# Seven block products move from the down-projection to 19 pairs of the up-projection, with two half-depth down units inside each step

## The reference, cut to what matters

```
h2 = rmsnorm(x, norm2_g)
up, new_conv_f = causal_dwconv(jnp.einsum('btd,df->btf', h2, w_up), ffn_conv0, conv_f_w, conv_f_b)
gf, vf = jnp.split(up, 2, axis=-1)
x = x + jnp.einsum('btf,fd->btd', jax.nn.gelu(gf) * vf, w_down)
```

## Time and profile before

| what | value |
|---|---|
| time, median of 3 runs | 1156.68 us (1156.22 to 1157.01) |
| time of the profiled execution | 1157.05 us |
| its span (first to last instruction or transfer) | 1155.3 us |
| TensorE busy | 1149.3 us, 99% of the span |
| VectorE busy | 663.3 us, 57% |
| ScalarE busy | 542.7 us, 47% |
| GpSimd busy | 245.5 us, 21% |
| feed-forward part on TensorE | from about 698 us to the end |

### The profile page before, as it was taken

The page is one execution under the profiler, slowest core; times in us unless marked ns, Lnnn a source line. Parts: engine busy times, 40 slices in busy tenths (PEclk is TensorE's granted clock), DMA queues, the critical chain, the costliest instruction groups (busy, mean ns, idle before and its releaser), DMA issues.

```text
span 1155.3 us, 21791 instructions
## 1 busy us (share of the span) xinstructions
PE 1149.3 (99%) x8865; PEld 1118.3 (97%) x8865; DVE 663.3 (57%) x1264; ACT 542.7 (47%) x991; POOL 245.5 (21%) x341
## 2 busy tenths in 40 slices
PE   9999999999999999999999999999999999999998
PEld 7999999999999999999999999999999999999998
DVE  7553543634622355665645557788757787667631
ACT  7444444444433357667533345445444545344422
POOL 2375153252330000000000025630006430000000
PEclk9999999999999999999999999999999999999999
DMA  8477245355331232222163227995548998422222
GB/s 245 143 214 179 80 136 158 92 141 140 103 106 56 76 89 74 74 77 63 54 200 96 72 68 244 184 176 150 174 119 240 189 159 237 124 83 83 82 84 59
DMA packets 212940, 147.97 MB, mean 128 GB/s; under 512 B 8906, under 2 KB 197966, under 8 KB 212858
## 3 DMA queue, kind: packets, MB, share of 16 engines
q1 hardware_dynamic: 176880, 97.83, 30.3%
q0 software_dynamic: 35888, 48.99, 19.6%
q10 hardware_dynamic: 90, 0.04, 0.0%
HBM read 136.79 MB, written 29.43 MB: 144 GB/s over the span
## 4 chain that ended last, share of the span: by engine, by line
PE 99%; DVE 1%; ACT 0%; issue 0%; DVEq 0%
PE ps L816 58%; PE ps L795 20%; PE ps L1117 8%; PE ps L1152 2%; PE ps L885 1%; PE ps L872 1%; PE ps L1035 1%; PE ps L928 1%; PE ps L953 1%; PE ps L949 1%; PE ps L897 1%; PE ps L959 1%; PE ps L913 1%; PE ps L916 1%; PE ps L838 0%; DVE w_s L1756 0%
## 5 line engine op out<-in xcount | busy, mean ns | idle before, releaser
L816 PE MATMUL ps<-h,w_s 128*128 128x288 f32 x3840 | 517.9, 296 | 0.0
L816 PEld LDWEIGHTS ps<-h,w_s 128*128 128x128 f32 x3840 | 512.6, 189 | 3.9 <-issue 3.9
L1750 DVE TENSOR_TENSOR w_s<-w_raw,w_s 128x1024 fp32r<-128x1024 f32 (+1 forms) x144 | 174.6, 1213 | 167.7 <-ACT w_s L1237 167.6
L1237 ACT ACTIVATE w_s<-w_raw 128x1024 fp32r<-128x1024 f32 (+1 forms) x144 | 149.3, 1037 | 161.7 <-PE ps L816 141.2
L795 PE MATMUL ps<-w_s,h 128*128 128x384 f32 x1152 | 217.4, 341 | 1.0 <-DVE w_s L1756 0.5
L795 PEld LDWEIGHTS ps<-w_s,h 128*128 128x128 f32 x1152 | 198.6, 188 | 2.9 <-DVE h L1777 0.7
L751 POOL DMA_DIRECT2D left_sums<-in_w_down x72 | 75.9, 2191 | 67.9 <-issue 43.1
L733 POOL DMA_DIRECT2D out<-f_row x6 | 3.4, 574 | 256.6 <-ACT f_row L1659 256.6
L1341 ACT ACTIVATE prob<-prob,stat 128x512 f32<-128x512 f32 (+1 forms) x20 | 15.2, 758 | 70.6 <-DVE stat L1908 70.6
L816 PE MATMUL ps<-mg_hi,w_s 128*128 128x288 f32 x256 | 46.5, 298 | 0.0
L1836 DVE TENSOR_REDUCE nrm<-sq 128x3 f32<-128x384 f32 (+1 forms) x40 | 22.0, 550 | 40.4 <-ACT sq L1294 34.9
(11 more groups left out here) (355 smaller groups left out, 1832.5 us busy)
## 6 DMA issues: line engine op xcount, KB each, us to landing
w_raw<-in_w_in SPq DMA_DIRECT2D x65, 512.0 KB, 3.9
w_raw<-in_w_up SPq DMA_DIRECT2D x48, 512.0 KB, 4.3
left_sums<-in_w_down POOLq DMA_DIRECT2D x72, 256.0 KB, 7.5
w_raw<-in_w_down SPq DMA_DIRECT2D x24, 512.0 KB, 4.2
sums<-left_sums SPq DMA_DIRECT2D x32, 256.0 KB, 3.4
kc<-in_cache_k_g POOLq DMA_DIRECT2D x48, 128.0 KB, 3.5
vc<-in_cache_v_g POOLq DMA_DIRECT2D x12, 512.0 KB, 6.4
w_raw<-in_w_out SPq DMA_DIRECT2D x8, 512.0 KB, 3.9
```

The lines of the kernel that those rows point to most:

```text
L816: last = mm(pu[u % 2][:, 512 * a:512 * a + HALF], w[:, part, k, :], x[:, k, HALF * a:HALF * (a + 1)], start=(k == 0 and i == 0), stop=(k = ...
L1237: A(w_s[:, ring(u), 0, 0:nkt[u], :], raw(u)[:, 0:nkt[u], :], ACT.Copy).then_inc(hi_ready, 1)
L1750: TT(w_s[:, ring(u), 1, 0:nkt[u], :], raw(u)[:, 0:nkt[u], :], w_s[:, ring(u), 0, 0:nkt[u], :], ALU.subtract).then_inc(lo_ready, 1)
```

## The change

The seven block products now serve the up-projection, and the down-projection is plain.

- Pairs 0 to 4 (`NSTD = 5`) are standard: 96 matmuls each. For pairs 5 to 23 (`NSEV = 19` steps) gate unit and value unit form the 2 x 2 block matrix: seven products, 84 matmuls. The right operands are blocks of the normed input and sums of them, formed once, in pairs 0 to 3 (`right_raw`, `right_hi`, `right_sums`, `right_lo`).
- The down-projection is cut into 48 units of half the depth (four depth tiles, 24 matmuls), in six rounds of eight. Two stand in each step: one between product 4 and product 5, one after product 7. Ten are left behind the last step.
- The weight-block sums: four copies, two adds from `w_up`, and two adds of sums to sums for each of 19 pairs, 152 DMAs. Most copies and the adds of the first ten pairs are issued in and around the recurrent branch, between the squarings.
- The convolution of the gate of a pair is done by VectorE at the start of the following step (`ffn_taps(i - 1, 0)`), and so are its gelu, its product and its split.
- There is no fourth slot for raw weights; one raw gate unit, one half value unit, four sums and four half down units take its place.

The diff, cut to its core:

```diff
+            def seven(s):
                 for n in range(1, 8):
+                    if n == 5:
+                        down(2 * s)
                     pe.wait_ge(st_lo, block_at(s, n))
                     if n == 1 and s:
-                        pe.wait_ge(st_ev, 5 * (s - 1) + 2)
+                        pe.wait_ge(st_ev, 4 * (s - 1) + 1)
...
                     if n in (3, 4):
-                        pe.wait_ge(st_cp, 2 * s + 1)
+                        pe.wait_ge(st_cp, 3 * s + 1)
                     if n == 5:
-                        pe.wait_ge(st_cp, 2 * s + 2)
+                        pe.wait_ge(st_cp, 3 * s + 3)
                     if n == 7:
-                        pe.wait_ge(st_ev, 5 * s + 3)
+                        pe.wait_ge(st_ev, 4 * s + 2)
...
+            pairs(1, NSTD - 1)
+            for s in range(NSEV):
+                seven(s)
+                r, q = divmod(s + NSTD, PPR)
+                if r and q == 0:
+                    state_rows(r - 1, s)
+                down(2 * s + 1)
+            for d in range(2 * NSEV, LAST):
+                down(d)
+            last_round_begin()
...
+            # ScalarE, the last standard pairs and a step
+            for i in range(NSTD):
+                pads_of(i)
+                for j in range(2):
+                    if i < NSTD - 1:
+                        hi_split(up_unit(i) + j + 2)
+                    elif j == 0:
+                        for n in FIRST_BLOCKS[:5]:
+                            block_hi(0, n)
+                    else:
+                        block_hi(0, 6)
+                        block_hi(0, 7)
+                    first_tap(i, j)
...
+                g_part(i)
+                state_taps(i)
+            for s in range(NSEV):
+                i, more = NSTD + s, s + 1 < NSEV
+                pads_of(i)
+                if s == 0:
+                    down_hi(0)
+                seed(s, 0)
...
+            # VectorE, a step
+                if s:
+                    ffn_taps(i - 1, 0)
+                    down_take(2 * s - 1)
...
+                down_take(2 * s)
+                val_added(s, 1)
...
+            ffn_taps(NPAIR - 1, 0)
+            product(NPAIR - 1)
+            g_rest(NPAIR - 1)
+            for d in range(2 * NSEV - 1, ND - 1):
+                down_take(d)
+                if d == 2 * NSEV - 1:
+                    down_lo(d + 2)
...
+            # GpSimd, between the squarings of the recurrent branch
+            left_landed(40)
+            left_adds(0, 3)
+            square(2)
+            left_adds(3, 7)
+            square(3)
...
+            # SP
+            sp.wait_ge(lo_ready, parts(U_ALL - 1))
+            load_gate(0)
+            for d in range(2):
+                load_down(d)
```

825 lines of the change are left out of this document (400 added, 425 removed).

## The result

The changed kernel takes **1162.68 us** (median of 20 executions), the kernel before 1156.69 us (20 executions, 1155.86 to 1158.53). The ratio is 1.0051 with a 95% interval of 1.0036 to 1.0065: slower by half a per cent, where 1150.0 us was forecast with a range of 1143 to 1158. The executions also differ far more than before. They run from 1155.85 to 1169.80 us, spread over the whole stretch, where those of the kernel before lie within 2.7 us. The execution that was profiled is the quickest of them (1155.85 us, span 1153.8), so its trace shows what is lost even in the best case, and not what is lost often.

A forecast was written before the change was run, and what follows sets the result against it. TensorE, busy 99% of the span, was taken as the bound. The terms -17.6 + 7.2 + 1.6 + 2.1 = -6.7 us took the profiled 1157.05 to 1150.35, a median of 1150.0 us, range 1143 to 1158.

The forecast's parts named there:

- Part 6: GpSimd's earlier queue in the recurrent branch: squarings come no later than now, costed at nothing.
- Part 3: Entrance to the block-product steps: TensorE waits for step 0's gate load and the tail behind it, +7.2 us.
- Part 1: Matmuls of up- and down-projection: 132 fewer at 0.133 us each, -17.6 us.
- Part 2: Steady step of 17.6 us: VectorE (14.1) and ScalarE (9.2) keep TensorE fed, costed at nothing.
- Rival D: VectorE sets the step and product 7 waits in all 19 steps, slower, 1169 us at 1 us beyond; chance 0.08.
- L: Landing time of step 0's gate load at the entrance, taken as 8 us; TensorE stands L - 0.8 us.
- Rival A: Cheap entrance: gate load lands in 4.1 us between accumulating DMA batches, clock stays up, 1144.8 us; chance 0.15.
- E - 10.1: Issue time of step 0's gate load, 10.1 us before E, the end of the last standard unit.
- Rival B: Steps 0 and 1 starve as loads land in 12 us, losing 2 to 6 us more, 1152 to 1156; chance 0.11.
- Part 4: TensorE's clock falls after the entrance stall, one product at double length, +1.6 us.
- Part 5: End: TensorE waits 2.0 us for down unit 39's low part on VectorE, plus 0.1 at the output transposes.
- the sum of -6.7 us: Whole kernel: matmuls -17.6, entrance +7.2, clock +1.6, end +2.1 us.

The follow-up runs named there:

- experiment 9: Changed kernel with plain copies and late third and fourth sums spread out, plus new orders at the up-projection's entrance and the end: 1140.18 us, ratio 0.9856.
- experiment 10: Changed kernel with plain copies and late third and fourth sums spread out and the new order at the end, entrance order unchanged: 1145.84 us, ratio 0.9903.
- experiment 11: Changed kernel with only the late third and fourth sums spread out, one each in steps 0 to 8: 1156.18 us, ratio 0.9994.
- experiment 12: Changed kernel with only the plain copies spread out, one pair's four copies per weight unit: 1158.75 us, ratio 1.0010.
- experiment 5: Changed kernel with GpSimd's late third sums held until the gate weights of steps 0 and 1 have landed: 1160.27 us, ratio 1.002.
- experiment 7: Changed kernel with 16 copies behind the branch weights, new order at the end, and late third sums behind the gate loads: 1153.88 us, ratio 0.9977.
- experiment 8: Changed kernel with copies behind branch weights, late third sums behind gate loads, and new orders at end and entrance: 1155.01 us, ratio 0.9985.
- experiment 1: Changed kernel with 16 plain copies moved behind the branch weights, to about 610 us: 1160.40 us, ratio 1.0035.
- experiment 4: Kernel before with 16 plain copies of 256 KB, read by nobody, added on GpSimd's queue in the changed kernel's places: 1163.92 us, ratio 1.0054.
- experiment 3: Changed kernel with only the order at the end altered, so down unit 39's parts come ahead of pair 23's: 1155.59 us, ratio 0.9995.
- experiment 2: Changed kernel with only the entrance order altered, first seed copy and early down unit parts moved ahead: 1159.62 us, ratio 1.0024.
- experiment 6: Changed kernel with step 0's gate load issued only after the first two late third sums have landed: 1170.40 us, ratio 1.0127.

## Why the prediction was wrong

Two steps failed, for one reason. Part 6 put the DMAs that GpSimd issues earlier at nothing, and they cost 6.1 us beside branch A's weights. Part 3 took one landing time, 8 us and at most 10, for the gate load, and it lands in 4 us or in 12 to 14. Both times loads on SyncE's queue are late beside a dense run of DMAs on GpSimd's.

**Part 1, the matmuls, was right.** 132 fewer, and experiment 9, where the waits are gone, is 16.6 us below the kernel before, against 17.6 by the sum. Two waits of 0.2 us that the kernel before does not have account for 0.4 of the 1.0 us between them. The two profiled executions (1157.05 and 1139.46 us) differ by 17.6.

**Part 2, the steady step, was right.** Product 1 comes at 845.50 and at 863.09 us in two following steps (17.59 us), with no idle time between. 960 to 1107 us holds 1106 to 1108 matmuls in the traces of experiments 9 to 12. Rival D, VectorE as the bound, did not happen.

**Part 3, the entrance, had the right formula and a wrong L.** "Even if the load is no hindrance" it gave 3.3 to 3.7 us, and 3.64 was measured in the kernel after; experiment 10 has the same 3.6 us. The longer case is borne out too: L - 0.8 is 13.1 for L = 13.9, and experiment 12 shows 7.00 + 3.42 us of idle time and some 2.6 us of slow products between, 13.0. What failed is the choice of one L. I took 8 from the landings beside accumulating adds. But the DMAs that run at this moment are the third sums, which add sums to sums and which no row showed beside a load of 512 KB; and L is not one number but 4 or 12 to 14, by a few us of relative timing. The upper bound of 10 for L, from which the range was made, was too low by 4. The statement that 36 DMAs run through until about 790 us was wrong as well: the last is issued at 785.8 us, but GpSimd has four gaps of 5 to 14 us between the batches. In the one of 5.35 us ahead of the third sums it waits for the adds to land, and the quick landing falls there. Rival A said so and got 0.15; its clock that stays up did not come. (The issue time, E - 10.1, was right, 10.2 in the traces, though its own terms, 0.8, 1.15 and 0.5 from E - 12.8, give 10.35.) Rival B's mechanism (later loads of steps 0 and 1 late) is what experiments 5, 7 and 8 turned up once the first collision was out of the way.

**Part 4, the clock, was close.** Experiments 9 and 10 differ by the entrance's order alone: 5.66 us, of which 3.63 is idle time, so the clock and what hangs on it costs 2.0, against 1.6 forecast. From the start of product 3 to that of product 5 it is 6.38 us in experiment 9, 7.97 in experiment 10 and 8.86 in the kernel after, so the slow products alone cost 1.6 and 2.5. A collision adds two more products at half clock.

**Part 5, the end, was short by nearly half.** The idle time is 1.84 us against 2.0 forecast. The slow clock behind it was given nothing, and cost about 1.6 in this trace: 60 matmuls take 9.88 us, and 8.36 in experiment 12 (the whole stretch differs by 1.6). The sentence on the Trainium skill in Part 4 ("TensorE: Matmul & The Clock Gate", Part 1) said that both stalls would pay by its rule. That goes beyond the page, by which the clock falls only after a longer idle time than the 1.84 us measured here. The trace of the changed kernel departs from the page and bears out the reading; as the last section shows, others don't.

**Part 6, GpSimd's earlier queue, is the step that failed outright.** "I cost it at nothing" looked at one thing, whether squarings come late, and that was right: they stay 20.55 us apart (461.15, 481.70, 502.25), even where the queue blocked for 9.94 us.

```profile
461.15 1.19 POOL L707 TENSOR_TENSOR a<-a_a 128x600 f32<-128x600 f32 x1 [12.30 <-ACT a_a L1515]
462.28 5.90 POOL L681 DMA_DIRECT2D left_sums<-in_w_up  x5
478.12 3.51 POOL L681 DMA_DIRECT2D left_sums<-in_w_up  x3 [9.94 <-issue]
481.70 1.19 POOL L707 TENSOR_TENSOR a<-a_a 128x600 f32<-128x600 f32 x1
502.25 1.19 POOL L707 TENSOR_TENSOR a<-a_a 128x600 f32<-128x600 f32 x1 [12.37 <-ACT a_a L1515]
```

It did not ask what the moved DMAs do to *other* queues. The second reading of the input had filled the DMA engines to 0.95 of their share between 576 and 590 us before the change, and 16 copies were put on either side of it, with weights of branch A due. That costs 5.9 to 8.5 us in the traces that keep these copies, 6.1 in the quickest execution, and nothing in those of experiments 1 and 12, which move them. Put into the sum of -6.7 us, these 6.1 leave -0.6, no change; the collisions then make the kernel slower. The adds in the recurrent branch, about which I reasoned at length, cost nothing: from 440 to 560 us TensorE does 937 matmuls, as before.

The sum with the measured terms, for a quick execution: -17.6 + 6.1 (branch) + 7.0 (entrance with its clock) + 3.7 (end with its clock) = -0.8. The profiled execution came out 1.2 us below that of before. The median is 6.8 us above this execution, and experiment 11 takes 6.5 of them away, most of which I put down to the collisions of loads with the late sums. So the forecast of -6.7 missed 6.1 for the branch, 1.6 for the end, and some 5 for the collisions in the middle of the distribution, since it had 8.8 for an entrance that costs 7.0 in quick and about 14 in median executions.

## What to carry to other kernels

When a change moves DMAs, go through every other queue's loads that will be in flight beside them and compare their landing time with their slack; that the queue's own engine keeps its time says nothing. Here loads beside a long run of bulk DMAs landed 6 to 13 us late. That cost nothing where they had the slack, and 6 us and more where they had not, and moving a run mostly moved the stall. The same bytes, issued a few at a time and each group released by the progress of the consumer, cost nothing. When the same program's executions spread by a per cent, look for a load on the critical path whose landing time has two values.

## What the runs showed of the hardware that I had not expected

- A load of 512 KB on SyncE's queue took 3.9 to 4.1 us with no sums in flight and 12.4 to 13.9 us if it was issued 2 to 4 us behind the first of nine accumulating DRAM-to-DRAM DMAs of 256 KB on GpSimd's queue (11.2 us at 6 us behind). Beside 12 to 16 plain copies and the second reading of the input, loads of 256 and 512 KB took 14.1 to 17.0 us (medians of two, kernel after and experiment 4), beside the reading alone 8.9 and 6.7. A load that was issued 0.9 us *ahead* of the nine (757.36 against 758.23 us) was not slowed at all. The Trainium skill, "DMA: Bandwidth & Descriptors" (Queues, rings and completion order), says that each DMA engine takes turns between the queues it has work for, a packet at a time. A load that shares all 16 engines with another queue should then be slower by a factor and not blocked, and the traces show a factor of about 3 (12.4 to 13.9 against 3.9 to 4.1 us). They also fit the turns. In experiment 3, where plain copies run beside a load from 590 to 600 us, the two queues move nearly the same number of packets, but GpSimd's (q0) hold 3.3 KB each and SyncE's (q1) 0.5 KB (columns: packets, MB, share of the engines' time):

```profile
q0 software_dynamic: 925, 3.08, 88.3%
q1 hardware_dynamic: 927, 0.46, 16.6%
```

  So the loads get every second packet and an eighth of the bytes. Beside the third sums it is 1181 packets with 2.13 MB against 1312 with 0.66 MB (experiment 12, 752 to 765 us). Whether larger packets in the loads would make them land sooner was not tried.
- The lower clock after an idle time is not certain. The same idle time of 1.83 to 1.84 us before down unit 39 is followed by some 12 matmuls at half clock in the kernel after (60 matmuls in 9.88 us), and by none in experiment 12 (8.36 us):

```profile
1114.33 9.88 PE L1164 MATMUL ps<-g,h 128*128 128x288 f32 x60 [1.84 <-DVE h L2282]
```

```profile
1118.07 8.36 PE L1166 MATMUL ps<-g,h 128*128 128x288 f32 x60 [1.83 <-DVE h L2284]
```

  Experiments 2, 5 and 11 go with the first (granted clock 0.83 in the ten us concerned), 1 and 6 with the second (1.00). Idle times of 2.1 us and more brought the lower clock in all traces here, one of 0.64 us (805.13, product in 1.83 us) did not.
- The fall can come after the engine has started again: in experiment 10 the product right behind an idle time of 3.63 us takes 1.97 us, hardly longer than normal, and the one after it 3.08.

```profile
769.53 1.97 PE L1134 MATMUL ps<-t,blk_b 128*128 128x288 f32 x12 [3.63 <-ACT ps L1673]
771.31 3.08 PE L1134 MATMUL ps<-h,blk_b 128*128 128x288 f32 x12
```
